# The triangular inverse of a chunked delta-rule scan: 64x64 tiles in a loop against 32x32 tiles written out, with VectorE transposes

## The chip, the cores and the metric

The kernel runs on one core of one Trainium2 chip. The metric is the device time of one execution in microseconds (us). A core has five engines with instruction streams of their own: PE (TensorE, matrix products, which writes PSUM), DVE (VectorE), ACT (ScalarE), POOL (GpSimd) and SP, which here only issues transfers. They meet through semaphores.

## The reference, cut to what matters

The reference is a two-layer hybrid block, then one layer of a second kind (differential attention, a recurrent scan in two directions, and an expert lookup). The change is in the scan alone:

```python
def wkv_scan(s0, scan_in):
    def step(s, inp):
        w, kk, a, k, v, r = inp
        sa = jnp.einsum('dbhij,dbhj->dbhi', s, kk)
        s = s * w[..., None, :] - sa[..., :, None] * (kk * a)[..., None, :] + v[..., :, None] * k[..., None, :]
        return s, jnp.einsum('dbhij,dbhj->dbhi', s, r)
    return lax.scan(step, s0, scan_in)
```

There are 2 directions `d`, 16 heads of width 64, and 256 context plus 256 input tokens, all in float32.

## The kernel before

The scan goes in 8 steps `h` of 64 tokens, steps 0 to 3 over the context and 4 to 7 over the input (`X_STEPS`, which also give outputs). Inside a step the token-by-token recurrence is a triangular system: for each direction and head a 64x64 matrix (I + L), L strictly triangular in time, has to be inverted. The 16 heads lie as 8 column groups `c` times two `head` halves of 64 partitions, so all matrices of a direction fill 128 partitions x 512 columns (8 blocks of 64 columns) of one buffer: `LT` holds the transposed system less the unit matrix, `Dm` the inverse as it grows, `DTm` its transpose (with the two heads' halves swapped), `ARm` the product in between.

The inverse doubles the size of its finished diagonal blocks by levels m = 1, 2, 4, 8, 16, 32 (`LEVELS` = 6). A level has for each direction a "left" product LT' x Dm on PE, a multiplication by a mask on DVE (`tt`, line 2431, reading PSUM), and two products on PE: one gives the new inverse, the other its transpose. Both are copied out of PSUM: lines 2308 and 2312 on ACT, line 2715 on DVE. The first level needs no product: POOL masks it (`begin_inverse`), and ACT makes its transposed copy (`first_transposed`, lines 2298 and 2299). PE's five other levels are a hardware loop (`pe.Fori`, line 1920) with one body of 96 `tile` calls, executed 5 times a step; direction 0 and 1 alternate, so that one's evacuation lies beside the other's products. All matmuls of the scan pass through `mm` (line 1597), therefore have that line; a `tile` call is one 64x64 product.

Around the inverse PE has, written out: `together` (removal and key products), `first_left`, `uncorrected`, then `inverse`; in the next step `corrected_values`, `state_update`, and with outputs `first_outputs`, `last_outputs` and `reads`. The order of each engine is the order of the program text; nothing is scheduled. PSUM banks go through two rings, `act_ring` and `dve_ring`, of four banks each; the inverse holds four banks of the first (`open(pe, "held")`), which needs ACT to have emptied its last two (`evac("U0", ...)`, line 2250).

Of the kernel before, what the change touches and what calls it, by code (L numbers as in the profile page):

```python
# [77 lines left out]
def layout(fields):  # L78
# [10 lines left out]
        ("level", 6 * 128), ("iota16", 16), ("heads", 4)]  # L89
# [38 lines left out]
def constants2():  # L128
# [20 lines left out]
    for m in (1, 2, 4, 8, 16, 32):  # L149
        same = (s[:, None] // (2 * m) == s[None, :] // (2 * m)) & (s[:, None] // m != s[None, :] // m)  # L150
        levels.append(before & same[:, None, :])
    put("level", -1.0 * np.tile(np.stack([m | np.eye(64, dtype=bool)[:, None, :] for m in levels], 1), (2, 1, 1, 1)))
# [178 lines left out]
def build_program(nc, W1, V1, K1, W2_all, VV2, K2, R2, PU, PV, xin, cin, out):  # L331
# [1058 lines left out]
    P_AT, LEVELS = slots_at + 4 * 1024, 6  # L1390
# [25 lines left out]
    def ch2(ap):  # L1416
        return ap.rearrange("p (d c n) -> p d c n", d=2, c=8)

# [90 lines left out]
    inverse_full, inverseT_full = signal("inverse_full", 2 * LEVELS - 2), signal("inverseT_full", 2 * LEVELS - 2)  # L1509
    inverse_ready = signal("inverse_ready", 2 * LEVELS - 2)  # L1510
    inverseT_ready = [signal(f"inverseT_ready{d}", LEVELS - 1) for d in range(2)]
    inverse_done = signal("inverse_done", 2)
# [71 lines left out]
    def _(pe):  # L1584
# [222 lines left out]
        def corrected_values(h, values_of=None):  # L1807
# [3 lines left out]
            for d in range(2):  # L1811
                pe.wait_ge(*inverse_done.at(h, d))
                pe.wait_ge(*u0_ready.at(h, d))
                for c in range(8):
                    for head in range(2):
                        last = tile(b[d], d, c, head, 1, 0, half_of(DTm), half_of(U0))
                        if values_of is not None and c < 7:
                            tile(turned[d], d, c, head, 0, 1, values(values_of), unit)
# [74 lines left out]
        def uncorrected(h):  # L1893
# [4 lines left out]
            for c in range(8):  # L1898
                for head in range(2):
                    tile(b[1], 1, c, head, 0, 1, half_of(Pm), half_of(St), c == 0, False)  # L1900
                    last = tile(b[0], 0, c, head, 1, 1, half_of(Apk), half_of(VT_TOK), c == 0, False)
            pe.wait_ge(*intra_ready.at(h, 1))
            pe.wait_ge(term_full.sem, mark(last))
            for c in range(8):
                for head in range(2):
                    first = tile(b[0], 0, c, head, 0, 1, half_of(Pm), half_of(St), False, True)
                    last = tile(b[1], 1, c, head, 1, 1, half_of(Apk), half_of(VT_TOK), False, True)
            first.then_inc(act_ring.full, 1)
            last.then_inc(act_ring.full, 1)

        def first_left(h, d, left):
            pe.wait_ge(*inverse_begun.at(h, d))
            for c in range(8):
                for head in range(2):
                    last = tile(left[d], d, c, head, 0, 0, half_of(LT), lambda side, d, c: C2["id2"][64 * side:64 * side + 64, :])
            last.then_inc(left_full.sem, 1)

        def inverse(h, left):
            products = [[act_ring.open(pe, "held") for _ in range(2)] for _ in range(2)]
            with pe.Fori(0, LEVELS - 1) as j:  # L1920
                for d in range(2):
                    pe.wait_ge(inverse_ready.sem, j * 2 + ((2 * LEVELS - 2) * h + d + 1))
                    pe.sem_inc(pe_step, 1)
                    for c in range(8):
                        for head in range(2):
                            last = tile(left[d], d, c, head, 0, 1, half_of(LT), half_of(Dm))
                    last.then_inc(left_full.sem, 1)
                for d in range(2):
                    pe.wait_ge(left_ready.sem, j * 2 + ((2 * LEVELS - 2) * h + d + 1))
                    pe.wait_ge(inverseT_ready[d].sem, j + ((LEVELS - 1) * h + 1))  # L1930
                    pe.sem_inc(pe_step, 1)
# [181 lines left out]
    def _(act):  # L2113
# [162 lines left out]
        def token_major_parts(h):  # L2276
# [10 lines left out]
            if h not in X_STEPS:  # L2287
                first_transposed(h, 0)
            removal_tokens(h, 1)
            key_tokens(h, 1)  # L2290
            if h in X_STEPS:
                first_transposed(h, 0)
            first_transposed(h, 1)

        def first_transposed(h, d):
            act.wait_ge(*inverse_begun.at(h, d))
            half = slice(512 * d, 512 * d + 512)
            A(DTm[64:128, half], ARm[0:64, half], ACT.Copy)
            A(DTm[0:64, half], ARm[64:128, half], ACT.Copy)
            act.drain().then_inc(inverseT_ready[d].sem, 1)  # L2300

        def inverse(h):
            banks = act_ring.held(4)
            for j in range(1, LEVELS):
                for d in range(2):
                    if j < LEVELS - 1:
                        act.wait_ge(*inverse_full.at(h, 2 * (j - 1) + d))
                        A(Dm[:, d * 512:(d + 1) * 512], banks[2 * d], ACT.Copy)
                        act.drain().then_inc(inverse_ready.sem, 1)
                    if j == LEVELS - 1 or d == 0:  # L2310
                        act.wait_ge(*inverseT_full.at(h, 2 * (j - 1) + d))
                        A(DTm[:, d * 512:(d + 1) * 512], banks[2 * d + 1], ACT.Copy)
                        act.drain().then_inc((inverse_done if j == LEVELS - 1 else inverseT_ready[d]).sem, 1)
# [107 lines left out]
    def _(v):  # L2421
# [160 lines left out]
        level = C2["level"].rearrange("p (m d t) -> p m d t", m=6, d=2)  # L2582
# [121 lines left out]
        def inverse(h, between):  # L2704
            left, banks = dve_ring.held(2), held_products[h]
            for j in range(LEVELS):
                for d in range(2):
                    if j == 1:
                        v.wait_ge(*inverseT_ready[d].at(h))
# [392 lines left out]
```

## Time and profile before

| | |
|---|---|
| three runs | 2724.05 us median (2721.91 to 2724.41) |
| profiled execution | span 2720.9 us from first to last instruction; no time of its own is given beside the span |
| busy | PE 92%, PE weight loads 63%, DVE 47%, ACT 22%, POOL 19% |
| granted TensorE clock | 0.974 of full over the span |
| the scan | about 1513 to 1888 us of the span |
| instruction transfers (queue q8) | 126 packets, 2.06 MB in the span |

Busy time says how long an engine had an instruction in flight; matmuls are pipelined, so a busy PE isn't PE at its peak. "issue" is idle time for which the profile shows no releaser. The instruction transfers are what brings the engines' programs from memory while they run: 16384 bytes a packet on q8.

### The profile page before, as it was taken

Reading aid. Unit: us, or ns where it says so; the run is one execution under the profiler, and the core shown is the slowest. Engines: PE = TensorE matmul, PEld = TensorE weight load, DVE = VectorE, ACT = ScalarE, POOL = GpSimd, SP = SyncE. Lnnn points to the kernel's source line nnn. Section 1 sums busy time; section 2 is a strip of 40 time slices with the busy share of each in tenths; the row PEclk is TensorE's granted clock in tenths of the full one; section 3 lists DMA queues with packets and bytes.
Section 4 is the critical chain, followed back from the end, with each engine's and each line's share of the span. In section 5 each row is a group of like instructions: output and inputs, shape, how many; then the busy total and the mean of one; then the engine's idle time right before and its main releaser. Section 6 shows DMA issues by size and latency. Waiting matters only on the chain.

```text
span 2720.9 us, 51616 instructions
## 1 busy us (share of the span) xinstructions
PE 2497.1 (92%) x22056; PEld 1706.8 (63%) x22056; DVE 1275.3 (47%) x2865; ACT 598.1 (22%) x1349; POOL 508.4 (19%) x418
## 2 busy tenths in 40 slices
PE   8999999999999999998899988899998988777777
PEld 6688786476886853444677888888866533333333
DVE  2873310037732101146447444444128667777765
ACT  1243000013330000114333444332002111111111
POOL 0000000000000000000012555430003455544552
PEclk9999999999999999999999999999999988988999
DMA  5333343344233335423453111003348999999997
GB/s 186 150 121 124 129 152 152 133 166 155 106 124 139 148 151 212 171 93 124 155 196 83 25 26 34 18 14 122 124 170 329 414 418 421 421 421 422 422 421 308
DMA packets 91234, 523.81 MB, mean 193 GB/s; under 512 B 39728, under 2 KB 39728, under 8 KB 43440
## 3 DMA queue, kind: packets, MB, share of 16 engines
q0 software_dynamic: 39360, 277.51, 25.0%
q1 hardware_dynamic: 51696, 243.80, 24.1%
q8 instruction: 126, 2.06, 0.3%
q14 instruction: 52, 0.43, 0.0%
HBM read 511.85 MB, written 9.44 MB: 192 GB/s over the span
## 4 chain that ended last, share of the span: by engine, by line
PE 70%; DVE 10%; DMA 10%; issue 3%; PEld 3%; ACT 2%; DVEq 1%; POOL 1%; ACTq 0%; PEldq 0%; SPq 0%; POOLq 0%
PE psum L523 35%; PE psum L1597 25%; DMA mem<-weights,mem 9%; PE psum L2055 5%; DVE mem L2924 4%; PEld psum L1597 3%; PE psum L765 2%; PE psum L539 1%; DVE mem L2431 1%; PE psum L2027 1%; DVEq L2552 1%; PE psum L1607 1%; POOL mem L3068 1%; DMA mem<-weights 0%; DVE mem L2568 0%
## 5 line engine op out<-in xcount | busy, mean ns | idle before, releaser
L523 PE MATMUL psum<-mem 128*128 128x256 f32 (+10 forms) x4248 | 954.8, 397 | 7.5 <-DVE mem L1079 3.3
L1597 PE MATMUL psum<-mem 64*64 64x64 f32 (+5 forms) x16032 | 899.8, 258 | 60.8 <-issue 25.6
L1597 PEld LDWEIGHTS psum<-mem 64*64 64x64 f32 (+2 forms) x16032 | 708.6, 144 | 251.3 <-issue 168.0
L523 PEld LDWEIGHTS psum<-mem 128*128 128x128 f32 (+5 forms) x4248 | 692.0, 182 | 262.6 <-issue 168.2
L2055 PE MATMUL psum<-mem 128*128 128x512 f32 x1024 | 497.7, 644 | 123.5 <-ACT mem L2395 121.3
L2055 PEld LDWEIGHTS psum<-mem 128*128 128x128 f32 x1024 | 206.5, 206 | 408.1 <-issue 246.0
L3068 POOL DMA_INDIRECT mem<-weights,mem x256 | 320.3, 1251 | 525.1 <-PE psum L2055 261.2
L2924 DVE CUSTOM_DVE_ANT_0 mem<-mem 128x1024 f32<-128x1024 f32 x256 | 307.4, 1224 | 139.8 <-DMA mem<-weights,mem 133.1
L2431 DVE TENSOR_TENSOR mem<-psum,mem 128x512 f32<-128x512 f32 (+1 forms) x193 | 130.6, 683 | 266.9 <-PE psum L1597 240.4
L2974 POOL TENSOR_TENSOR mem<-mem 128x512 f32<-128x512 f32 (+2 forms) x132 | 168.7, 1294 | 201.0 <-DVEq L2677 150.8
L2431 DVE TENSOR_TENSOR mem<-mem 128x512 f32<-128x512 f32 (+7 forms) x211 | 136.6, 655 | 89.2 <-ACTq L2163 67.5
L2390 ACT ACTIVATE mem<-mem 128x4 f32<-128x4 f32 (+2 forms) x70 | 14.3, 205 | 511.6 <-DVE mem L2928 511.6
L1284 DVE TENSOR_TENSOR mem<-mem 128x512 f32<-128x512 f32 x32 | 22.1, 692 | 193.7 <-ACTq L982 193.7
L1071 DVE SCALAR_TENSOR_TENSOR mem<-mem 128x256 f32<-128x256 f32 x240 | 105.6, 481 | 9.4 <-issue 0.9
L1287 DVE TENSOR_TENSOR mem<-psum,mem 128x512 f32<-128x512 f32 x8 | 5.5, 692 | 205.6 <-PE psum L523 205.6
L1304 POOL DMA_DIRECT2D mem<-vectors x1 | 0.5, 537 | 540.0 <-DVEq L1291 540.0
L1306 POOL MEMSET mem<- 128x256 f32 x1 | 0.3, 311 | 493.9 <-ACT mem L985 493.9
L3031 POOL DMA_DIRECT2D rates_dram<-mem x16 | 14.2, 892 | 406.3 <-DVEq L2600 406.3
L2395 ACT ACTIVATE mem<-mem 128x128 f32<-128x128 f32 x256 | 82.5, 390 | 32.7 <-DVE mem L2431 31.3
L837 ACT ACTIVATE mem<-psum 128x512 f32<-128x512 f32 (+4 forms) x88 | 45.6, 569 | 104.4 <-PE psum L523 100.2
L981 ACT ACTIVATE mem<-psum 128x512 f32<-128x512 f32 x32 | 19.1, 597 | 201.5 <-PE psum L523 201.5
L765 PE MATMUL psum<-mem 128*128 128x512 f32 x128 | 55.8, 594 | 3.8 <-DVEq L1273 3.8
(244 smaller groups left out, 1304.7 us busy)
## 6 DMA issues: line engine op xcount, KB each, us to landing
mem<-weights SPq DMA_DIRECT2D x100, 2048.0 KB, 7.4
rates_dram<-mem POOLq DMA_DIRECT2D x16, 512.0 KB, 4.9
mem<-rates_dram SPq DMA_DIRECT2D x32, 256.0 KB, 4.5
mem<-weights SPq DMA_DIRECT2D x7, 1024.0 KB, 6.8
mem<-weights SPq DMA_DIRECT2D x2, 2176.0 KB
mem<-weights,mem POOLq DMA_INDIRECT x256, 27.4
mem<-weights SPq DMA_DIRECT2D x2, 1536.0 KB, 8.2
mem<-weights SPq DMA_DIRECT2D x2, 1152.0 KB
```

The lines of the kernel that those rows point to most:

```text
L523: ins = pe.matmul(out, lhsT, rhs, start=start, stop=stop, skip_group_check=skip)
L539: last = pe.transpose(b[0:rows_, at:at + n], src, ident[0:n, 0:n])
L765: ins = pe.matmul(b, mg[:, k, t * P:(t + 1) * P], w[half][:, k, :], start=k == 0, stop=k == 7)
L837: return A(dst, src(b) if src else b, func).then_inc(act_ring.free, 1)
L1071: v.scalar_tensor_tensor(cacc[:, c, :], src, w, cacc[:, c, :], ALU.mult, ALU.add)
L1597: ins = pe.matmul(out, lhsT, rhs, start=start, stop=stop, skip_group_check=skip)
L2055: last = pe.matmul(psum[:, 4 + 2 * t + half, :], diag[:, n % DIAGS, :], rows_uv[buf_of[n]][:, D + half * 512:D + (half + 1) * 512], start= ...
L2395: A(diag[:, n % DIAGS, :], ident, ACT.Copy, scale=g1[:, n:n + 1]).then_inc(diag_ready.sem, 1)
L2431: return v.tensor_tensor(o, a, b, op)
L2924: v.tensor_tensor_reduce(u, u, h2[:, t, :], 1.0, 0.0, ALU.mult, ALU.add, actp[:, n:n + 1])
L2974: return pool.tensor_tensor(o, a, b, op)
L3068: pool.indirect_dma_start(out=rows_uv[buf_of[n]], out_offset=None, in_=UV, in_offset=bass.IndirectOffsetOnAxis(ap=eidx_u[:, n:n + 1], axis ...
```

## The change

The last level (m = 32) is taken out of the doubling. The first five (`LEVELS` = 5) act within 32x32 diagonal blocks, so each of them is done on 32x32 tiles: `block_products` makes four calls of `mm` a column group (two heads times two blocks) where `tile` made two, each with 32 rows, 32 columns of weights and 32 moving columns. The buffers `Db`, `DbT` and `ARb` are half as wide (128x256 a direction). The transpose of the inverse, before a second product with a copy out of PSUM, is now a DVE 32x32 transpose of `Db`. PE's loop is gone: its four remaining passes are a Python `for`, written out. The off-diagonal 32x32 block comes from a cross part: two products in a row, with copies by ACT between and behind, and DVE copies of the finished diagonal blocks into `DTm`. `first_transposed` on ACT and POOL's second instruction in `begin_inverse` are gone. `DTm` and `VT_TOK` products keep to their own half (`swapped` arguments 0 in place of 1).

```diff
@@ PE
         def first_left(h, d, left):
             pe.wait_ge(*inverse_begun.at(h, d))
             for c in range(8):
-                for head in range(2):
-                    last = tile(left[d], d, c, head, 0, 0, half_of(LT), lambda side, d, c: C2["id2"][64 * side:64 * side + 64, :])
+                last = block_products(left[d], d, c, block_in(LT, 0), block_unit)
             last.then_inc(left_full.sem, 1)
 
+        def block_products(bank, d, c, lhsT, rhs, block=(0, 1), crossed=0, at=0):
+            for head in range(2):
+                for n in block:
+                    rows_ = block_rows(head, n)
+                    last = mm(bank[block_rows(head, n ^ crossed), at + 32 * c:at + 32 * c + 32],
+                              lhsT(rows_, n, d, c), rhs(rows_, n, d, c), True, True, skip=True)
+            return last
...
-            with pe.Fori(0, LEVELS - 1) as j:
+            for j in range(LEVELS - 1):
                 for d in range(2):
-                    pe.wait_ge(inverse_ready.sem, j * 2 + ((2 * LEVELS - 2) * h + d + 1))
-                    pe.sem_inc(pe_step, 1)
+                    pe.wait_ge(*inverse_ready.at(h, 2 * j + d))
                     for c in range(8):
-                        for head in range(2):
-                            last = tile(left[d], d, c, head, 0, 1, half_of(LT), half_of(Dm))
+                        last = block_products(left[d], d, c, block_in(LT, 0), block_of(Db))
                     last.then_inc(left_full.sem, 1)
                 for d in range(2):
...
                     for c in range(8):
-                        for head in range(2):
-                            one = tile(products[d][0], d, c, head, 1, 0, half_of(DTm), half_of(ARm))
-                            two = tile(products[d][1], d, c, head, 1, 1, half_of(ARm), half_of(DTm))
-                    one.then_inc(inverse_full.sem, 1)
-                    two.then_inc(inverseT_full.sem, 1)
+                        last = block_products(products[d][0], d, c, block_of(DbT), block_of(ARb))
+                    last.then_inc(inverse_full.sem, 1)
+            for d in range(2):
+                pe.wait_ge(*inverse_ready.at(h, 2 * LEVELS - 2 + d))
+                for c in range(8):
+                    last = block_products(products[d][1], d, c, block_in(LT, 1), block_of(Db), (1 - lower(d),), 1)
+                last.then_inc(cross_full.sem, 1)
+            for d in range(2):
+                pe.wait_ge(*cross_ready.at(h, d))
+                pe.wait_ge(*inverseT_ready[d].at(h, LEVELS - 1))
+                for c in range(8):
+                    block_products(products[d][1], d, c, block_of(ARb), block_of(DbT), (lower(d),), 1, at=256)
+                    last = block_products(products[d][1], d, c, block_of(Db), block_unit, (lower(d),), 0, at=256)
+                last.then_inc(cross_full.sem, 1)
@@ ACT
-            first_transposed(h, 1)
...
         def inverse(h):
             banks = act_ring.held(4)
             for j in range(1, LEVELS):
                 for d in range(2):
...
+                    act.wait_ge(*inverse_full.at(h, 2 * (j - 1) + d))
+                    A(Db[:, d, :, :], blocks(banks[2 * d]), ACT.Copy)
+                    act.drain().then_inc(inverse_ready.sem, 1)
@@ DVE
-                    tt(dir_(ARm if j else Dm, d), left[d].rearrange("p (c n) -> p c n", c=8), bc(level[:, j, 1 - d, :], 1, 8), ALU.mult)
+                    tt((ARb if j else Db)[:, d, :, :], blocks(left[d]), bc(level[:, j, 1 - d, :], 1, 8), ALU.mult)
                     v.drain().then_inc((left_ready if j else inverse_ready).sem, 1)
-                if 0 < j < LEVELS - 1:
-                    v.wait_ge(*inverseT_full.at(h, 2 * (j - 1) + 1))
-                    v.tensor_copy(DTm[:, 512:1024], banks)
-                    v.drain().then_inc(inverseT_ready[1].sem, 1)
+                for d in range(2):
+                    if j:
+                        v.wait_ge(*inverse_ready.at(h, 2 * j + d))
+                    v.transpose(DbT[:, d, :, :], Db[:, d, :, :])
+                    v.drain().then_inc(inverseT_ready[d].sem, 1)
                 between(j)
```

PE's program for the inverse of step 1 before, from the last `first_left` to the end of the loop; the loop body stands once in the program and is executed five times. "x15" behind a row is how often it follows itself, the names in brackets are semaphores.

```order
L1597 MATMUL psum<-mem 64x64 [waits inverse_begun,qt_ready]
L1597 MATMUL psum<-mem 64x64 x15
L1920 UNCONDITIONAL_BRANCH [waits act_bank_free]
L1920 ISA
L1597 MATMUL psum<-mem 64x64 [waits inverse_ready]
L1597 MATMUL psum<-mem 64x64 x15
L1922 REGISTER_ALU
L1597 MATMUL psum<-mem 64x64 [waits inverse_ready]
...
L1597 MATMUL psum<-mem 64x64 [waits left_ready,inverseT_ready1]
L1597 MATMUL psum<-mem 64x64 x31
```

The same place in the changed program, from `first_left` through the first of the four passes, which all read like it, and then the cross part.

```order
L1607 MATMUL psum<-mem 32x32 [waits inverse_begun,qt_ready]
L1607 MATMUL psum<-mem 32x32 x31
L1607 MATMUL psum<-mem 32x32 [waits act_bank_free,inverse_ready]
L1607 MATMUL psum<-mem 32x32 x31
...
L1607 MATMUL psum<-mem 32x32 [waits inverseT_ready1,left_ready]
L1607 MATMUL psum<-mem 32x32 x31
...
L1607 MATMUL psum<-mem 32x32 [waits inverse_ready]
L1607 MATMUL psum<-mem 32x32 x15
L1607 MATMUL psum<-mem 32x32 [waits inverse_ready]
L1607 MATMUL psum<-mem 32x32 x15
L1607 MATMUL psum<-mem 32x32 [waits inverseT_ready0,cross_ready]
L1607 MATMUL psum<-mem 32x32 x31
```

A pass is now 128 matmuls in the text, in place of one body of 96 for all five passes; `first_left` has 32 a direction in place of 16, and the cross part adds 96. Counted over the whole program, the scan has 8064 matmuls in the text, before 3712; the branch is gone.

ACT's program before the inverse of step 0, before: the two rows of line 2298 and 2299 twice, ahead of the `evac("U0")` rows of line 2250.

```order
L2262 ACTIVATE mem<-psum 128x512 [waits intra_ready,act_bank_full]
L2298 ACTIVATE mem<-mem 64x512 [waits inverse_begun]
L2299 ACTIVATE mem<-mem 64x512
L2262 ACTIVATE mem<-psum 128x512 [waits lt_ready]
...
L2250 ACTIVATE mem<-psum 128x512 [waits act_bank_full] x2
```

And in the changed program (line 2298 is there `token_half`, line 2286 `evac`, line 2331 the copy of `Db`):

```order
L2298 ACTIVATE mem<-psum 128x512 [waits intra_ready,act_bank_full]
L2298 ACTIVATE mem<-psum 128x512 [waits lt_ready]
L2298 ACTIVATE mem<-psum 128x512 [waits intra_ready,act_bank_full]
L2286 ACTIVATE mem<-psum 128x512 [waits act_bank_full] x2
L2251 ACTIVATE mem<-mem 128x1024 [waits k_ready,rates_landed1]
L2253 ACTIVATE mem<-mem 128x16x64
L2331 ACTIVATE mem<-psum 128x256 [waits inverse_full] x8
```

The copies of the transposed first level no longer stand ahead of `evac("U0")`.

## Rows read from the trace of the kernel before

**Rows 1.** The page: engines, chain by line, largest group, instruction queue
```profile
PE 2497.1 (92%) x22056; PEld 1706.8 (63%) x22056; DVE 1275.3 (47%) x2865; ACT 598.1 (22%) x1349; POOL 508.4 (19%) x418
...
L1597 PE MATMUL psum<-mem 64*64 64x64 f32 (+5 forms) x16032 | 899.8, 258 | 60.8 <-issue 25.6
```

**Rows 2.** Windows, the scan: us, then busy us (instructions), clock, DMA
```profile
1513.00:1888.00 375.00, 332.33 (x13473) 315.44 (x13474) 166.23 (x242) 152.47 (x243) 151.53 (x117) 0.98 0.14 38
```

**Rows 3.** Windows, four loop passes of step 1's inverse
```profile
1571.31:1575.77 4.46, 4.38 (x216) 4.16 (x211) 2.07 (x3) 1.64 (x3) 4.29 (x4) 1.00 0.00 0
...
1584.64:1589.07 4.43, 4.30 (x206) 4.12 (x201) 2.33 (x5) 1.76 (x3) 0.00 (x0) 1.00 0.00 0
sum 17.76, PE 17.16 PEld 16.41 DVE 8.55 ACT 6.98 POOL 8.45; mean PE 4.29 PEld 4.10 DVE 2.14 ACT 1.75 POOL 2.11
```

**Rows 4.** Chain, first pass of that loop: start us, us, what
```profile
1571.79 2.08 PE psum L1597 x64
1573.87 0.07 issue
1573.94 2.09 PE psum L1597 x128
1576.04 0.22 issue
```

**Rows 5.** Transfers by queue, the scan
```profile
q8 instruction: 59, 0.97, 1.1%
```

**Rows 6.** Transfers, 1615 to 1632 us, in 40 slices
```profile
DMA packets 0, 0.00 MB, mean 0 GB/s; under 512 B 0, under 2 KB 0, under 8 KB 0
```

**Rows 7.** Transfers, 1817 to 1833 us, in 40 slices of 0.4 us
```profile
GB/s 0 41 0 0 0 0 0 0 0 0 41 0 0 0 0 0 0 0 0 41 0 0 0 0 0 0 0 0 41 0 0 0 0 0 0 0 41 0 0 0
DMA packets 5, 0.08 MB, mean 5 GB/s; under 512 B 0, under 2 KB 0, under 8 KB 0
```

**Rows 8.** Transfers, 1772 to 1800 us, in 40 slices of 0.7 us
```profile
GB/s 23 0 0 0 0 23 0 0 0 0 0 23 0 0 0 0 23 0 12 0 0 23 0 12 0 0 0 23 0 0 0 0 23 0 0 0 0 23 0 0
q8 instruction: 8, 0.13, 2.0%
```

**Rows 9.** Timeline of PE, 1815 to 1845 us
```profile
1820.06 6.65 PE L1597 MATMUL psum<-mem 64*64 64x64 f32 x254 [0.25 <-issue]
1827.15 3.27 PE L1597 MATMUL psum<-mem 64*64 64x64 f32 x126 [0.45 <-issue]
1830.73 3.11 PE L1597 MATMUL psum<-mem 64*64 64x128 f32 x126 [0.32 <-issue]
1834.25 0.97 PE L1597 MATMUL psum<-mem 64*64 64x64 f32 x49 [0.41 <-issue]
1835.37 1.40 PE L1597 MATMUL psum<-mem 64*64 64x64 f32 x77
1840.59 4.72 PE L1597 MATMUL psum<-mem 64*64 64x64 f32 x111 [3.83 <-issue]
```

**Rows 10.** Waits in the scan: waiter, releaser, us, times, longest us
```profile
PE psum L1597 <- ACT mem L2250: 10.2, 4, 2.6
```

**Rows 11.** Timeline ahead of step 3's inverse
```profile
1647.24 0.63 ACT L2298 ACTIVATE mem<-mem 64x512 f32<-64x512 f32 x1
1647.88 0.63 ACT L2299 ACTIVATE mem<-mem 64x512 f32<-64x512 f32 x1
...
1648.61 1.31 ACT L2250 ACTIVATE mem<-psum 128x512 f32<-128x512 f32 x2
...
1650.36 0.94 PE L1597 MATMUL psum<-mem 64*64 64x64 f32 x18 [2.51 <-ACT mem L2250]
```

**Rows 12.** Groups of the scan: busy us, mean ns, idle before
```profile
L2431 DVE TENSOR_TENSOR mem<-psum,mem 128x512 f32<-128x512 f32 x166 | 113.4, 691 | 154.3 <-PE psum L1597 150.5 <-issue 2.0
L2308 ACT ACTIVATE mem<-psum 128x512 f32<-128x512 f32 x64 | 38.2, 597 | 95.0 <-PE psum L1597 92.0
L2431 DVE TENSOR_TENSOR mem<-mem 128x512 f32<-128x512 f32 (+2 forms) x18 | 21.7, 1221 | 1.8 <-issue 0.7
```

**Rows 13.** The same by form: PE's weight loads and matmuls
```profile
L1597 PEld LDWEIGHTS psum<-mem 64*64 64x64 f32 x13408 | 303.1, 137 | 58.5 <-issue 50.0 <-PE psum L1597 3.3 <-ACTq L2274 1.5
L1597 PE MATMUL psum<-mem 64*64 64x64 f32 x12416 | 286.0, 223 | 38.4 <-issue 19.9 <-ACT mem L2250 10.2 <-PE psum L1597 1.2
...
L1597 PE MATMUL psum<-mem 64*64 64x128 f32 x992 | 38.7, 271 | 4.7 <-issue 4.6
```

More of the change, by code:

```diff
@@ L148, in constants2 @@
     levels = []
-    for m in (1, 2, 4, 8, 16, 32):
+    for m in (1, 2, 4, 8, 16):
         same = (s[:, None] // (2 * m) == s[None, :] // (2 * m)) & (s[:, None] // m != s[None, :] // m)
-        levels.append(before & same[:, None, :])
-    put("level", -1.0 * np.tile(np.stack([m | np.eye(64, dtype=bool)[:, None, :] for m in levels], 1), (2, 1, 1, 1)))
+        level = before & same[:, None, :] | np.eye(64, dtype=bool)[:, None, :]
+        levels.append(np.concatenate([level[:32, :, :32], level[32:, :, 32:]], 0))
+    put("level", -1.0 * np.tile(np.stack(levels, 1), (2, 1, 1, 1)))
     put("iota16", np.tile(np.arange(16), (P, 1)))
@@ L1417, in ch2, with blocks, lower @@
         return ap.rearrange("p (d c n) -> p d c n", d=2, c=8)
+    Db, DbT, ARb = (ap.rearrange("p (d c n) -> p d c n", d=2, c=8) for ap in (Dm[:, 0:512], Dm[:, 512:1024], ARm[:, 0:512]))
+    def blocks(bank):
+        return bank[:, 0:256].rearrange("p (c n) -> p c n", c=8)
+    def lower(d):
+        return 1 - d
     gsig2 = sb2(2048, rtop[0] - 4096).rearrange("p (c t) -> p c t", c=DC)
@@ L1815, in corrected_values @@
                     for head in range(2):
-                        last = tile(b[d], d, c, head, 1, 0, half_of(DTm), half_of(U0))
+                        last = tile(b[d], d, c, head, 0, 0, half_of(DTm), half_of(U0))
                         if values_of is not None and c < 7:
@@ L1905, in uncorrected, with block_rows, block_of, block_in @@
                 for head in range(2):
-                    first = tile(b[0], 0, c, head, 0, 1, half_of(Pm), half_of(St), False, True)
-                    last = tile(b[1], 1, c, head, 1, 1, half_of(Apk), half_of(VT_TOK), False, True)
+                    first = tile(b[0], 0, c, head, 0, 0, half_of(Pm), half_of(St), False, True)
+                    last = tile(b[1], 1, c, head, 1, 0, half_of(Apk), half_of(VT_TOK), False, True)
             first.then_inc(act_ring.full, 1)
             last.then_inc(act_ring.full, 1)
+        def block_rows(head, block):
+            return slice(64 * head + 32 * block, 64 * head + 32 * block + 32)
+        def block_of(buf):
+            return lambda rows_, block, d, c: buf[rows_, d, c, :]
+        def block_in(buf, side):
+            return lambda rows_, block, d, c: ch2(buf)[rows_, d, c, 32 * (block ^ side):32 * (block ^ side) + 32]
+        def block_unit(rows_, block, d, c):
+            return C2["id2"][rows_, 32 * block:32 * block + 32]
+        def block_products(bank, d, c, lhsT, rhs, block=(0, 1), crossed=0, at=0):
[5 more added lines that the diff above has]
+            return last
         def first_left(h, d, left):
@@ L2305, in inverse @@
                 for d in range(2):
[L2306 to L2313, printed above, removed]
+                    act.wait_ge(*inverse_full.at(h, 2 * (j - 1) + d))
+                    A(Db[:, d, :, :], blocks(banks[2 * d]), ACT.Copy)
+                    act.drain().then_inc(inverse_ready.sem, 1)
+            for d in range(2):
+                act.wait_ge(*cross_full.at(h, d))
+                A(ARb[:, d, :, :], blocks(banks[2 * d + 1]), ACT.Copy, scale=-1.0)
+                act.drain().then_inc(cross_ready.sem, 1)
+            for d in range(2):
+                act.wait_ge(*cross_full.at(h, 2 + d))
+                A(ch2(DTm)[:, d, :, 32 * lower(d):32 * lower(d) + 32], blocks(banks[2 * d + 1][:, 256:512]), ACT.Copy)
+                act.drain().then_inc(cross_ready.sem, 1)
             act.sem_inc(act_ring.full, 4)
@@ L2748, in next_rates @@
                     chunk_decay(h + 1)
+            if h == 0:
+                v.memset(DTm, 0.0)
+                v.drain()
             inverse(h, next_rates)
@@ L3016, in begin_inverse @@
         def begin_inverse(h):
-            first = C2["level"].rearrange("p (m d t) -> p m d t", m=LEVELS, d=2)[:, 0, :, :]
             for d in range(2):
```

52 lines of the change are left out of this document (20 added, 32 removed).

## The prediction

> **What bounds the kernel now.** I read the page first: PE is busy 92% of the span and the scan's line 1597 is a third of that, mostly 64x64 tiles [rows 1]. The change touches the scan alone, so I cut it out: 375 us in which PE is busy 332, DVE 166, ACT 152, at a clock of 0.98 [rows 2]. Inside it stand two kinds of PE code, and they are paced by different things.
>
> What is one `tile` call to the engine? By the text the scan executes 3712 matmuls once and the 96 of the body four more times in 8 steps, 6784 in all. The trace has 13408 weight loads and 12416 + 992 matmuls on 64x64 tiles [rows 13], that is two of each for a float32 call, less 1% of missing records. So a call is four instructions. 3712 calls are 14848 instructions; at 64 bytes these are 58 packets of 16384 bytes, and the scan has 59 [rows 5]. The packets are PE's program. In seventeen microseconds of loop none comes at all [rows 6]: a loop runs on what is there.
>
> The written-out code. In 1817 to 1833 us (`first_outputs` to `reads` of the last step) a packet comes every 9 slices of 0.4 us, four gaps in 35 slices: 3.5 us each [rows 7]. In 1772 to 1800 us there are eight, seven gaps in 37 slices of 0.7 us: 3.7 us [rows 8] (the two slices of half height are others'). PE runs in the same beat: 126 matmul records (with their loads 252 instructions, about a packet), a gap with "issue" as its reason, 126 more, and once 3.83 us of nothing [rows 9]. It could go faster: 128 records with their loads, 256 instructions, take 2.09 us in the loop [rows 4]. So written-out tile code here costs about 3.6 us per 256 instructions, not 2.1. Before the change the loop shields the densest part of the scan from that.
>
> **The change part by part.** First the instructions. The text of the scan grows from 3712 to 8064 calls: a step gains 32 in `first_left`, 4 passes x 128 in place of one body of 96, and 96 in the cross part, 544 x 8 = 4352 calls = 17408 instructions = 68 packets.
>
> (1) Removed: four of the five executions of the body in each step, 32 x 4.44 = 142.1 us.
>
> (2) Added: 68 packets of straight code. Bounds per packet: 2.09 us if the program were always there [rows 4]; 3.5 us the quiet beat [rows 7]; 3.7 us in 1772 to 1800 [rows 8]; and 3.95 us as the mean of all written-out scan code with every other wait in it, (375 - 142) / 59 [rows 2, 5]. Inside the inverse the other waits are few, so I take 3.6: 68 x 3.6 = +244.8 us.
>
> (3) The body's first execution stays in the sum as 384 instructions, a packet and a half. It lasts 4.44 us now and will be paced as well: 1.5 x 3.6 = 5.4, +1.0 a step, +8 us.
>
> (4) ACT's copies of the transposed first level go. Ahead of the inverse ACT does two of 0.63 us a direction and only then the `evac("U0")` that frees the banks [rows 11]; PE waits for exactly that 10.2 us, four times up to 2.6 [rows 10], in steps 0 to 3. This wait should vanish, but a gap in PE also lets a packet arrive, so part comes back as pacing: I take -8 (bounds 0 and -10.2).
>
> (5) DVE: eight masks of 0.69 us become halves of that width; the copies become two transposes of 128x256 a pass. No trace row shows a DVE transpose; below, half of a 0.69 us tensor_tensor, 0.35; above, the 1.22 us of one four times as wide [rows 12]. Even so a pass holds 2 x 0.4 + 2 x 1.22 = 3.2 us of DVE against a pass of 2 packets, 7.2 us: nothing. ACT's copies halve too (0.60 to some 0.35) [rows 12]. The four small DVE copies, the memset of step 0, and POOL's dropped instruction lie beside PE. At the cross part PE waits one ACT copy (0.35 and its way) between the products of one direction, with the other's 64 or 128 instructions ahead of it: under 1 us, inside the packet's pace. `corrected_values` now shares the array better with the values' tiles, but it is 256 instructions and so a packet anyway: 0.
>
> Sum: -142.1 + 244.8 + 8 - 8 = **+103 us**. The profiled execution has no time of its own; its span of 2720.9 stands 3.2 under the median of the runs, and I take that margin as unchanged: 2720.9 + 102.7 + 3.2 = **2827 us**, +3.8%.
>
> One rule is weighed here. The trace shows the beat and the gaps [rows 7, 9]. The Trainium skill (Runtime: NRT & Kernel Launch, Instruction fetch mechanics) says that the sequencer streams the program in blocks of 16 KiB (256 instructions), prefetching while it executes, and that crossing a block is "mostly hidden", so that kernels do well to unroll. The block size agrees with the 58 and 59 packets above; the hiding doesn't agree with [rows 9]. By the page the sum would be that of the first rival.
>
> **The rivals.**
> *Fetch hidden, faster.* The dense inverse gets its instructions at the rate of the loop. Then 256 instructions last 2.09 us [rows 4]: a pass of 512 takes 4.2, four 16.7; the cross part 384 instructions, 3.1 plus some 1.0 of turns through ACT; `first_left` 1.0 more. 21.8 against 5 x 4.44 = 22.2 a step, -3; the ACT wait -10.2; and corrected values with free positions, up to -1.4 in seven steps. About -20: 2704 us. For it: nothing shows a packet late in the loop. Against it: [rows 9]. It decides from where a packet costs less than (142.1 + 10) / 68 = 2.2 us; the mean gaps are 3.5 and 3.7, and the shortest one in [rows 7] is 8 slices, 3.2 us.
> *Narrow tiles twice as fast as well.* If besides 32 columns let a stage of 128 instructions end in half its 1.04 us, 16 stages save another 8.3 us a step: some 2640 us. The second stage of [rows 4] speaks against it: with twice the instructions it takes as long as the first, at 8.2 ns an instruction, and their number doesn't fall.
> *The clock drops.* PE waits longer, and the granted clock falls to the lower level, 1.2 GHz, for much of the scan. The paced 32x32 code would hardly mind. The 57 packets of 64x64 work would: 2.09 us of array time doubles to 4.2, past 3.6, +0.6 each, +34: 2861 us. Against: with the gaps of [rows 9] the scan still had 0.98 [rows 2].
> *The stream is slower than its beat*, since transfers of rates and weights crowd it in the inverse, where the loop used to hide that; at 4.2 us a packet, +41: 2868 us.
> *Chain through DVE.* If a transpose took over 3 us a pass would wait for it; 2 us more in 32 passes is +64, 2891 us. Nothing near it in [rows 12].
>
> **How the numbers follow.** Chances: paced at 3.4 to 3.95 us, 0.82; hidden 0.04; hidden and faster tiles 0.01; clock 0.04; slower stream 0.05; DVE chain 0.01; the rest, 0.03, is a partly hidden stream between 2725 and 2790. The likeliest case's bounds: 68 x 3.4 (a tenth under [rows 7]) = 231, less 142.1, less 10.2, is +79, 2803; 68 x 3.95 = 269, less 142.1, plus 8, is +135, 2859. To leave no more than 2 in 10 out I take a little more below, for a stream that gets ahead in PE's other waits: **2795 to 2864**. A measurement here can't tell less than 0.2% (5 us) from no change. Faster by over 0.2%: 0.05; within: 0.01; slower: 0.94.
>
> **What would show it.** In the profile after: q8 packets up by 68, from 126 to about 194; the scan at about 480 us in place of 375; in an inverse a packet every 3.5 to 3.7 us with no pause, some ten a step, a pass at about 7.2 us; PE's idle time before line 1607 "issue" and up by over 100 us; no wait for ACT's `evac` of 2.6 us; a DVE transpose of 0.3 to 1.2 us. Wrong it is if packets come closer than 3.4 us in the inverse (then the beat before was PE's demand, not a limit), if a pass is near 4.2 us, or if passes wait for DVE or ACT by name.

## The result, and the profile after

The changed kernel takes 2850.69 us median (2847.77 to 2852.27, four runs), the kernel before in the same measurement 2724.23 (2721.91 to 2728.85): a ratio of 1.0452, 95% interval 1.0438 to 1.0466. The forecast was 2827 in a range of 2795 to 2864. The profiled execution has a span of 2850.4 us.

The page of the changed kernel, to be read against [rows 1]: engines, granted clock in 40 slices, instruction queue, chain by engine, largest group.

```profile
PE 2482.6 (87%) x24616; PEld 1683.8 (59%) x24616; DVE 1266.1 (44%) x2930; ACT 547.8 (19%) x1301; POOL 486.2 (17%) x402
...
PEclk9999999999999999999997766666999999989999
...
q8 instruction: 194, 3.18, 0.5%
...
PE 64%; DVE 10%; DMA 10%; issue 9%; PEld 3%; ACT 1%; DVEq 1%; POOL 1%; ACTq 0%; PEldq 0%; SPq 0%; POOLq 0%
...
L1607 PE MATMUL psum<-mem 32*32 32x32 f32 (+8 forms) x18592 | 889.2, 264 | 202.2 <-issue 180.2
```

PE is busy for less time than before (2482.6 us against 2497.1) and the span is 130 us longer: the time is idle time of PE, 202.2 us ahead of the matmuls of the line that the scan uses where it was 60.8, and 180.2 of it has no releaser. The queue has 194 packets, 68 more. The windows of the scan up to 2004 us (12 us short of the place at which [rows 2] ends), and in it of one stretch of an inverse; the number behind the engines is the granted clock:

```profile
1513.00:2004.00 491.00, 306.29 (x15970) 284.58 (x15965) 146.47 (x301) 99.93 (x191) 130.81 (x101) 0.66 0.09 22
1586.00:1626.00 40.00, 23.49 (x1238) 22.36 (x1239) 8.19 (x21) 5.42 (x14) 11.05 (x8) 0.51 0.02 4
```

How much longer the scan is shows best at one instruction that both kernels have, VectorE's first behind the products of the last step, before and after:

```profile
1873.16 0.69 DVE L2431 TENSOR_TENSOR mem<-psum,mem 128x512 f32<-128x512 f32 x1 [6.83 <-PE psum L1597]
2001.01 0.69 DVE L2458 TENSOR_TENSOR mem<-psum,mem 128x512 f32<-128x512 f32 x1 [11.37 <-PE psum L1607]
```

It comes 128 us later, nearly the whole of the 130, and PE enters the scan at the same time (1513.01 and 1512.52 us). In the stretch of the inverse DVE (8.2 us of 40) and ACT (5.4) can't be what PE waits for in its 16.5 idle microseconds. PE's timeline there, start and length of each stretch of matmuls, in brackets the idle time before it:

```profile
1587.86 1.93 PE L1607 MATMUL psum<-mem 32*32 32x32 f32 x128 [1.96 <-issue]
1591.70 1.93 PE L1607 MATMUL psum<-mem 32*32 32x32 f32 x127 [1.91 <-issue]
1595.60 1.93 PE L1607 MATMUL psum<-mem 32*32 32x32 f32 x128 [1.97 <-issue]
1599.45 1.92 PE L1607 MATMUL psum<-mem 32*32 32x32 f32 x127 [1.92 <-issue]
```

This is [rows 9] again, but where the gaps before were 0.25 to 0.45 us, they are now as long as the work. 128 records of matmuls with their loads are 256 instructions, one packet; the starts lie 3.84 to 3.90 us apart. The transfers of 1585 to 1615 us, in slices of 0.75 us, have the same beat, a packet every fifth slice and once every sixth:

```profile
GB/s 22 0 0 0 0 22 0 0 0 0 22 0 0 0 0 22 0 0 0 0 22 0 0 0 0 22 0 11 0 0 0 22 0 0 0 0 22 0 0 0
...
q8 instruction: 8, 0.13, 2.3%
```

This stretch is a little slower than the rest. ACT's copies of one direction's inverse follow each other, over the eight steps, by 6.92 to 8.00 us, 7.52 on average: that is a pass of two packets, 3.76 us each.

The waits of the scan say the same by name; the last row is what is left of [rows 10]:

```profile
PE psum L1607 <- issue: 179.1, 109, 3.9
PE psum L1607 <- PE psum L1607: 2.0, 8, 0.8
PE psum L1607 <- ACT mem L2286: 1.9, 2, 1.0
```

### The profile page after: what moved, and what is told of

It reads as the page before. It is cut to its first block, busy times and chain, and to the rows that moved or that the text cites. A ratio compares the mean times of both kernels' runs of the same rounds, so it can differ in the third digit from the quotient of the medians.

```text
span 2850.4 us, 56438 instructions
## 1 busy us (share of the span) xinstructions
PE 2482.6 (87%) x24616; PEld 1683.8 (59%) x24616; DVE 1266.1 (44%) x2930; ACT 547.8 (19%) x1301; POOL 486.2 (17%) x402
## 4 chain that ended last, share of the span: by engine, by line
PE 64%; DVE 10%; DMA 10%; issue 9%; PEld 3%; ACT 1%; DVEq 1%; POOL 1%; ACTq 0%; PEldq 0%; SPq 0%; POOLq 0%
PE psum L524 33%; PE psum L1607 24%; DMA mem<-weights,mem 9%; DVE mem L2957 4%; PE psum L2091 3%; PEld psum L1607 3%; PE psum L766 2%; PE psum L540 1%; DVE mem L2458 1%; PE psum L2063 1%; POOL mem L3096 1%; PE psum L1617 0%; DMA mem<-weights 0%; DVEq L2579 0%; DVE mem L2595 0%
## 5 line engine op out<-in xcount | busy, mean ns | idle before, releaser
L1607 PE MATMUL psum<-mem 32*32 32x32 f32 (+8 forms) x18592 | 889.2, 264 | 202.2 <-issue 180.2
L1607 PEld LDWEIGHTS psum<-mem 32*32 32x32 f32 (+5 forms) x18592 | 688.3, 152 | 402.3 <-issue 319.6
L2091 PE MATMUL psum<-mem 128*128 128x512 f32 x1024 | 493.7, 639 | 128.9 <-ACT mem L2422 128.8
L2458 DVE TENSOR_TENSOR mem<-psum,mem 128x512 f32<-128x512 f32 (+2 forms) x177 | 98.1, 561 | 345.8 <-PE psum L1607 319.0
L3007 POOL TENSOR_TENSOR mem<-mem 128x512 f32<-128x512 f32 (+2 forms) x116 | 147.9, 1295 | 334.8 <-DVEq L2704 280.2
L2741 DVE STREAM_TRANSPOSE mem<-mem 128x256 f32<-128x256 f32 x80 | 35.6, 445 | 107.1 <-ACTq L2332 105.2
L2331 ACT ACTIVATE mem<-psum 128x256 f32<-128x256 f32 x64 | 24.6, 385 | 229.9 <-PE psum L1607 229.9
```

The lines of the kernel that those rows point to most:

```text
L1607: ins = pe.matmul(out, lhsT, rhs, start=start, stop=stop, skip_group_check=skip)
L2091: last = pe.matmul(psum[:, 4 + 2 * t + half, :], diag[:, n % DIAGS, :], rows_uv[buf_of[n]][:, D + half * 512:D + (half + 1) * 512], start= ...
L2458: return v.tensor_tensor(o, a, b, op)
L2741: v.transpose(DbT[:, d, :, :], Db[:, d, :, :])
L3007: return pool.tensor_tensor(o, a, b, op)
```

## The experiments

"Text" is here the program as it stands in memory. Theory: text that TensorE has not run before comes at 3.3 to 3.9 us for 256 instructions, whatever they do, and this sets the time wherever they could run faster. Rivals: the 32x32 tiles themselves are slow (dispatch, array, evacuation), or the lower clock is the cause, or the writing out costs in some other way. Each ratio is to the kernel before, in the same job.

**The loop back, 32x32 tiles kept.**

```diff
-            for j in range(LEVELS - 1):
+            with pe.Fori(0, LEVELS - 1) as j:
                 for d in range(2):
-                    pe.wait_ge(*inverse_ready.at(h, 2 * j + d))
+                    pe.wait_ge(inverse_ready.sem, j * 2 + (2 * LEVELS * h + d + 1))
+                    pe.sem_inc(pe_step, 1)
...
```

> The changed kernel with PE's four passes put back into a hardware loop, still on 32x32 tiles with transposes and the cross part. Pacing by instruction packets: 3 passes x 128 calls x 4 instructions x 8 steps = 48 packets leave the text, so 146 packets on q8; those 24 repeats then run at 3.7 to 4.4 us in place of 7.7 (two packets of 3.85), 2850 - 24 x (3.3 to 4.0) = 2755 to 2771 us, and the granted clock comes back to full in the loop. Rival, the narrow tiles or the lower clock themselves make a pass slow, or its chain through DVE and ACT: a pass stays at 7 us or more and the time above 2840.

Measured: 2733.7 us, ratio 1.0027 (1.0015 to 1.0039), 146 packets. 117 of the 126 us come back by the loop alone, so the tiles are not slow. The time is 21 us below the expected range. The granted clock did not come back to full in the loop as expected: it was 0.84 over the scan. PE's timeline at the loop of one step:

```profile
1575.23 3.82 PE L1607 MATMUL psum<-mem 32*32 32x32 f32 x256 [0.17 <-issue]
1579.23 3.01 PE L1607 MATMUL psum<-mem 32*32 32x32 f32 x256 [0.18 <-issue]
```

Each row is one pass, 256 records. The first ran at a granted clock of 0.50 and started 4.0 us before the next; the second ran at 0.99, and the next starts 3.3 us behind it. The last two passes of the eight loops take 3.37 us on average, 6.6 ns for each of 512 instructions, against 4.44 us of the 64x64 body and 8.2 ns in its second stage. So the tiles are faster than the theory had it, and in a loop, other than in the written-out kernel, the lower clock costs time (in the loops of the whole scan 128 records take 1.9 to 2.2 us at the lower level, 1.4 to 1.7 at the full one). From ACT's first copy of an inverse to its last, the eight steps together take 92 us in place of 181; from the last copy of one inverse to the first of the next, seven times, 244 us in place of 275. So a quarter of the 117 us lies outside the passes. One packet arrives on q8 while each loop runs, which may be what the text behind it gains; no run separates that.

**The loop written out, 64x64 tiles kept** (the same edit on the kernel before).

> The kernel before with its loop written out and nothing else changed: 64x64 tiles, five passes. Pacing: 48 more packets (174 in all), a pass is one and a half packets, 5.3 to 5.8 us in place of 4.44, so 2724 + 40 x (0.9 to 1.4) = 2760 to 2780 us. Rival, writing out is free and the narrow tiles are the cause: the branch's 0.25 us a pass is saved, 2715 to 2724 us.

Measured: 2770.5 us, 1.0161 (1.0140 to 1.0181), 174 packets, clock 0.973 of full, as before the change. Writing out costs 45 us here, with no new tile, no transpose and no lower clock.

**More work for each instruction.** A product moves 64 columns in place of 32; the second half is overwritten by the next column group.

```diff
+            w = 64 if c < 7 else 32
...
+                    last = mm(bank[rows_, 32 * c:32 * c + w], lhsT(rows_, n, d, c), flat[rows_, d, 32 * c:32 * c + w],
+                              True, True, skip=True)
```

> The changed kernel, with 64 moving columns in place of 32 in the products of the four passes; every column beyond the first 32 is overwritten by the next product. Twice the array work in the same number of instructions. Pacing: 194 packets, the same time within 10 us (2840 to 2860), gaps in PE shorter as it is busy for longer. If the lower clock in the inverse is what makes a packet 3.85 us there and not 3.5, and the wider products bring the clock back, some 80 packets x 0.35 less: about 2822 us. Rival, array work sets the passes: they get longer, above 2880 us.

Measured: 2843.0 us, inside the expected range, 1.0436 (1.0413 to 1.0459), an interval that overlaps the changed kernel's. PE's timeline in the inverse of this run:

```profile
1587.70 1.89 PE L1607 MATMUL psum<-mem 32*32 32x64 f32 x128 [1.43 <-issue]
1591.27 1.89 PE L1607 MATMUL psum<-mem 32*32 32x64 f32 x127 [1.68 <-issue]
1594.87 1.89 PE L1607 MATMUL psum<-mem 32*32 32x64 f32 x128 [1.70 <-issue]
1598.43 1.77 PE L1607 MATMUL psum<-mem 32*32 32x64 f32 x119 [1.68 <-issue]
```

A stretch of 256 instructions takes 1.89 us here and took 1.93 before, but not at the same clock: the granted clock is 1.00 in this timeline and was 0.50 in that of the changed kernel. Elsewhere in this run wide stretches at 0.50 show the array's work, and then the gaps shrink:

```profile
1650.04 3.42 PE L1607 MATMUL psum<-mem 32*32 32x64 f32 x127 [1.31 <-issue]
1654.15 3.42 PE L1607 MATMUL psum<-mem 32*32 32x64 f32 x128 [0.69 <-issue]
```

With 1.89 us of work at one level and 3.42 at the other, the beat stays at 3.6 to 4.1 us. The array isn't what paces, though at the lower clock twice the columns come close to it. The clock over the scan rose from 0.66 to 0.88, and the whole is 8 us shorter, which with overlapping intervals is no established gain.

**Half the text of the passes.** Column groups 4 to 7 are left out of the products, masks and copies of the four passes; half of the matrices are not inverted.

```diff
                     pe.wait_ge(*inverse_ready.at(h, 2 * j + d))
-                    for c in range(8):
+                    for c in range(4):
                         last = block_products(left[d], d, c, block_in(LT, 0), block_of(Db))
...
```

> The changed kernel with column groups 4 to 7 left out of the products of the four passes (half the matrices are not inverted), DVE's masks and ACT's copies halved with them; the waits, the stages and their order stay. Pacing: 32 packets fewer (162), a pass is one packet of 3.5 to 3.85 us, 2850 - 32 x 3.85 = 2727 us, at most 10 from it. Rival, a pass is set by its chain of four stages through PE, DVE and ACT with their hand-overs: it shortens only by the array time of half the products, 2850 - 32 x 1.7 / 1 = 2795 us or more.

Measured: 2728.6 us, 1.0017 (1.0000 to 1.0034), 162 packets. 32 packets fewer are worth 122 us, 3.8 each: the beat of the timeline. A turn through DVE and ACT, which has the same number of steps as before, is not what a pass waits for.

**The wait for ACT alone.** On the kernel before, the four copies of the transposed first level are moved behind `evac("U0")`.

```diff
-            first_transposed(h, 1)
...
                 act.drain().then_inc(u0_ready.sem, 1)
+            for d in range(2):
+                first_transposed(h, d)
```

> The kernel before with ACT's two transposed copies a direction moved behind its evacuation of U0, which frees the banks that the loop needs; nothing else. It sizes the term for ACT's wait by itself. The 10.2 us that PE waited for that evacuation in steps 0 to 3 go, if nothing else was late there: 2714 us. If a packet of instructions was on its way meanwhile, part stays as issue: 2718 to 2725. Rival, the copies come too late for the loop's first products, which take their place as the wait: no change, 2724 us or above.

Measured: 2725.9 us, 0.9999 (0.9990 to 1.0009): no change, as the rival expected. The waits of its scan:

```profile
PE psum L1597 <- issue: 34.7, 41, 3.5
PE psum L1597 <- DVEq L2709: 3.5, 4, 0.9
PE psum L1597 <- PE psum L1597: 1.2, 7, 0.2
```

No wait for `evac` is left of the 10.2 us of [rows 10], but 34.7 us have no releaser where [rows 13] had 19.9 ahead of the 64x64 matmuls and 4.6 ahead of the wider ones, and 3.5 are new on DVE (L2709 is the signal behind the mask of an inverse). No wait of PE names the late copies. So PE's time at this place isn't set by ACT's copies alone. That the new idle time is the wait for text, which the old wait had been hiding, is inferred from its having no releaser; the views don't name it.

**VectorE transposes without 32x32 tiles.** The loop over 64x64 tiles, its second product replaced by a DVE transpose of 128x512, with the cross part.

```diff
-                            one = tile(products[d][0], d, c, head, 1, 0, half_of(DTm), half_of(ARm))
-                            two = tile(products[d][1], d, c, head, 1, 1, half_of(ARm), half_of(DTm))
+                            last = tile(products[d][0], d, c, head, 0, 0, half_of(DTm), half_of(ARm))
...
```

> Transposes on VectorE and the cross part as in the changed kernel, but 64x64 tiles (block diagonal matrices) and the four passes in a hardware loop. Text: 32 + 64 + 96 calls a step in place of 128 before, so 8 packets more than before, 134, at 3.75 us each +30; 24 repeats of a pass of two stages of 32 calls. The stages have two of four array positions, so 1.04 us each and 4.4 a pass: 24 x 4.4 in place of 32 x 4.44, -36; ACT's wait up to -10. Sum 2708 to 2722 us. Rival, the chain through a full-width transpose and mask sets a pass, above 5 us: over 2735 us.

Measured: 2734.4 us, 1.0033 (1.0020 to 1.0046), 134 packets. Missed by 12 us, and within 1 us of the rival's mark. In a loop the transpose is not hidden. It takes 711 ns for 128x512, and PE waits 34 times for L2749, which is the signal behind the mask; the mask in turn stands behind two transposes in VectorE's order.

```profile
PE psum L1611 <- issue: 42.7, 39, 4.6
PE psum L1611 <- DVEq L2749: 22.5, 34, 1.4
...
L2753 DVE STREAM_TRANSPOSE mem<-mem 128x512 f32<-128x512 f32 x80 | 56.9, 711 | 50.0 <-ACTq L2344 48.1
```

The chain through one pass shows it:

```profile
1576.08 2.10 PE psum L1611 x64
...
1578.20 0.60 ACT mem L2343
...
1578.85 0.71 DVE mem L2753
...
1579.68 0.69 DVE mem L2470
...
1580.64 2.10 PE psum L1611 x64
```

Yet a pass lasts only 4.56 us (1576.08 to 1580.64) where 4.4 was expected, so over all 32 passes this is 5 us. The forecast also had up to 10 us for ACT's wait, which the run before showed to be worth nothing; without it the sum is 2718, and some 11 us stay open.

**Less text, with loops.** Four kernels take calls out of the straight part. The first two leave out the 32 unit products a step that carry the diagonal blocks through the cross part (DVE copies them instead):

```diff
-                    block_products(products[d][1], d, c, block_of(ARb), block_of(DbT), (lower(d),), 1, at=256)
-                    last = block_products(products[d][1], d, c, block_of(Db), block_unit, (lower(d),), 0, at=256)
+                    last = block_products(products[d][1], d, c, block_of(ARb), block_of(DbT), (lower(d),), 1, at=256)
```

With 32x32 tiles:

> The loop on 32x32 tiles (first experiment, 2734 us) without the 32 products with the unit matrix in each step's cross part; VectorE copies those finished diagonal blocks instead. 4 packets fewer, 142 on q8. Pacing: 4 x 3.75 = 15 us less, about 2719 us. Rival, only engine work counts, and the cross part waits for its copies anyway: the products took 0.85 us of PE a step at most, so 2727 us or no change.

Measured: 2723.9 us, 0.9989 (0.9977 to 1.0001), 142 packets; 10 us under the run with the loop back, between the two expectations. With 64x64 tiles:

> The kernel of loops over 64x64 tiles with VectorE transposes (2734.4 us, 134 packets) without the unit products of the first block copies, which VectorE makes. 32 calls a step fewer are 4 packets fewer (130 on q8). If each packet is worth 3.7 us, 2719 us; if only the wait of the passes for the VectorE transposes counts, which stays as it is (22 us in 34 waits), 2730 us or more.

Measured: 2718.9 us, 0.9974 (0.9962 to 0.9986), 130 packets, as the packets expect. The wait behind mask and transposes stayed (22.3 us in 33 waits), yet 15.5 us went.

The other two also take `first_left` off PE: GpSimd masks the first level into the transposed buffer, VectorE transposes it. The edit as the 32x32 kernel has it; with 64x64 tiles it is one mask into `DTm` and a transpose into `Dm`:

```diff
+                for n in range(4):
+                    rows_, at = slice(32 * n, 32 * n + 32), 32 * (n % 2)
+                    ptt(DbT[rows_, d, :, :], ch2(LT)[rows_, d, :, at:at + 32], bc(first[rows_, d, :], 1, 8), ALU.mult)
                 pool.drain().then_inc(inverse_begun.sem, 1)
...
+                v.wait_ge(*inverse_begun.at(h, d))
+                v.transpose(Db[:, d, :, :], DbT[:, d, :, :])
```

With 64x64 tiles:

> The loop on 64x64 tiles with transposes, without the unit products, and with the first level made by POOL's mask and a VectorE transpose in place of PE products with the unit matrix. Text: 64 + 64 calls a step, as many as before, so 126 packets; 24 repeats of 4.4 us. Pacing: 8 packets fewer than the kernel with transposes in the loop, 30 us: 2680 to 2695 us, faster than before by 30 to 45. Rival, the first level's way through POOL and VectorE lies open, some 2 us a step: 2700 to 2710 us.

Measured: 2712.6 us, 0.9961 (0.9946 to 0.9976), 126 packets. This is above both ranges, 2.6 us over the rival's: PE now waits for the first level's way through GpSimd and VectorE, 9.4 us in 4 waits at the head of an inverse, and 4 packets fewer than in the run before gained only 6 us. With 32x32 tiles:

> The kernel with loops over 32x32 tiles and without unit products (2723.9 us, 142 packets on q8), with the first level made from four masks of 32 partitions on GpSimd into the buffer DbT and a VectorE transpose, in place of 64 matmul calls a step. The theory that packets on TensorE's queue set the time expects 8 packets fewer (134 on q8) and about 3.7 us for each, so some 2694 us. The rival, that the way through GpSimd and VectorE opens at the head of an inverse (as the waits of 9.4 and 12.8 us did in the run of the 64x64 kernel without a first level on TensorE, 2712.6 us), expects 2703 to 2712 us, with a wait of PE or DVE for the masks or their transposes in the chain.

Measured: **2697.7 us**, 0.9899 (0.9885 to 0.9913), 134 packets: 1.0% under the kernel before and the fastest of all, 4 us from what the pacing theory expects and 5 below the rival's range. Its waits in the scan:

```profile
PE psum L1607 <- issue: 58.1, 63, 3.7
PE psum L1607 <- DVEq L2736: 10.1, 5, 2.1
PE psum L1607 <- ACT mem L2284: 5.4, 3, 1.8
```

The head of an inverse does wait here too (10.1 us; L2736 is the signal behind the transpose of the first level), but narrow transposes keep the passes free of VectorE.

**How much text may stand in a loop.** The four 32x32 passes as two executions of a body of two passes, 1024 instructions.

```diff
-            with pe.Fori(0, LEVELS - 1) as j:
-                for d in range(2):
+            with pe.Fori(0, (LEVELS - 1) // 2) as j:
+                for i in range(2):
+                    for d in range(2):
...
```

> The changed kernel with its four passes as a hardware loop of two passes a body, executed twice: 1024 instructions in the body, where the loop of one pass has 512 (2733.7 us, 146 packets) and the written-out program 2048 (2850.7 us, 194 packets). The text grows by 128 calls a step over the loop of one pass, 512 instructions, 16 packets in all. If each packet of text brought costs what the 48 of the full writing out cost, (2850.7 - 2733.7) / 48 = 2.44 us, this run has 162 packets and some 2773 us. If the body no longer fits into what PE keeps of its program, it is brought for each execution: 194 packets and some 2850 us. A rival in which writing out costs by something else than the text (the waits with constants, the loop's increments) expects 2734 us.

Measured: 2778.4 us, 1.0189 (1.0175 to 1.0204), 162 packets; forecast 2773. One inverse on PE's timeline:

```profile
1580.77 1.95 PE L1607 MATMUL psum<-mem 32*32 32x32 f32 x125 [2.00 <-issue]
1584.57 1.95 PE L1607 MATMUL psum<-mem 32*32 32x32 f32 x126 [1.85 <-issue]
1588.29 2.06 PE L1607 MATMUL psum<-mem 32*32 32x32 f32 x126 [1.77 <-issue]
1592.40 6.92 PE L1607 MATMUL psum<-mem 32*32 32x32 f32 x484 [2.05 <-issue]
1599.74 3.52 PE L1607 MATMUL psum<-mem 32*32 32x32 f32 x282 [0.42 <-DVEq L2740]
```

Here both regimes stand side by side. The first execution of the body limps, 126 records and 1.8 to 2.0 us of nothing. From its last hundred records on, through the branch and most of the second execution, 484 records run in 6.92 us without a break. Same instructions and the same engines beside them, and much the same granted clock (0.54 over the three slow stretches, 0.59 over the fast one): the difference is whether the text has been there.

## Why the prediction was right, point by point

*What bounds the kernel, and step (2)*, hold. 68 packets were forecast and 68 came; removing text in the passes (3.8 us a packet for 32) and keeping it in a loop (117 us for 48) move the time, and more array work for each instruction doesn't. The size was short: 3.6 us was taken from two windows of straight code, where the packets of [rows 2] that come within 4.3 us of each other lie 3.75 us apart on average, and the passes of the changed kernel ran at 3.76 a packet (7.52 us a pass where 7.2 were forecast). Steps (2) and (3) together price 68 + 12 = 80 packets, so this is 13 us. With the 8 us of step (4), below, it makes 21 of the miss of 24 us.

*Step (1)*, 142 us removed, can't be seen alone, but it fits: the scan ended 128 us later, and -142 + 80 x 3.76 - 8 x 4.44, the last for the first execution that step (3) prices anew, = +123. The forecast for the scan was about 480 us; 375 and 128 are 503.

*Step (3)*, the first execution paced as well, is what the timeline of the loop of two passes shows.

*Step (4)* failed: the wait for ACT was given -8 and is worth nothing. It went (10.2 to 1.9 us), but the run that took it away alone was no faster (0.9999), and idle time without a releaser had taken its place there. Its bound of 0 was the right value; the doubt stood in the step ("part comes back as pacing"), only the part was all.

*Step (5)* holds in the written-out kernel: the transpose takes 445 ns, inside its bounds of 0.35 and 1.22, and no wait of PE names DVE.

```profile
L2741 DVE STREAM_TRANSPOSE mem<-mem 128x256 f32<-128x256 f32 x80 | 35.6, 445 | 107.1 <-ACTq L2332 105.2
L2458 DVE TENSOR_TENSOR mem<-psum,mem 128x256 f32<-128x256 f32 x80 | 34.0, 425 | 108.5 <-PE psum L1607 107.1
L2331 ACT ACTIVATE mem<-psum 128x256 f32<-128x256 f32 x64 | 24.6, 385 | 229.9 <-PE psum L1607 229.9
```

The cover of that zero was the slow text: with 64x64 tiles in a loop the wider transposes stand in the chain of every pass, and a pass lasts 4.56 us. The 2 us a pass of the last rival are far from it.

*The rivals.* That the text is hidden (2704 us) is out by every written-out run. That narrow tiles are faster as well was half right as a mechanism and had no effect: 3.37 us a pass against 4.44, seen only in a loop. The prediction's argument against it, 8.2 ns an instruction whatever the tile, is refuted by 6.6 ns.

The clock did fall, as the third rival said, which had a chance of 0.04: the granted clock of the scan was 0.66 in place of 0.98, its lower level of 1.2 GHz for some 41 us in each inverse, after PE had begun to idle for half of its time. That it would hardly touch the paced 32x32 code was right too. Stretches of 256 instructions took 1.93 us there, and between packets closer than 4.3 us in the scan the mean was 3.77 us at the lower level (77 of them) and 3.75 at the full one (20): the text, not the clock, paces. The +34 of this rival rested on 64x64 work outside the inverse, where the clock had mostly recovered. No run changes the clock alone; what these show is that the packets came no slower at the lower level.

Of the signs of being wrong one came in part: 8 of the 126 intervals between packets were under 3.4 us (the shortest 3.30). The mean stood well above it.

*The rule of the Trainium skill* (Runtime: NRT & Kernel Launch, Instruction fetch mechanics) that crossing a block is "mostly hidden", and that kernels prefer full unrolling where possible (for the sake of its taken branches, not of the crossing, as the prediction puts it), goes against these runs where the instructions are short: unrolled, the same passes cost 45 us (64x64) and 117 us (32x32). Its size of a block agrees: 16384 bytes a packet, 256 instructions.

**What stays open.** Why a packet takes what it takes was not settled: 3.75 us on average in the scan of both kernels, 3.84 to 3.90 in the stretch shown, 3.63 in the run with wide products at the full level. Nor does a packet have one price: 3.8 us where text of the passes went with its work, 2.8 and 2.3 where text replaced executions of a loop (45 us for the first 16 packets, 72 for the next 32), since the loop's executions took time as well. In the four kernels with less text it was 2.4 to 3.9 a packet except from 130 to 126, where 6 us came for four. Whether the new wait at the head took the rest there was not tested.

## What to carry to other kernels

Count the instructions of a written-out stretch and divide by 256: where that many packets at some 3.7 us exceed its work, the text is the bound, and neither smaller tiles nor faster helpers gained anything here. Put such stretches in a hardware loop, even one of two executions, and take out calls that only copy; a float32 call costs four instructions on 32x32 tiles as on 64x64. The best kernel here is only 1.0% under the one before, so look first at what share of the whole such stretches have. A wait that ends while the next packet is still on its way may be worth nothing, so price a removed wait together with what paces the engine next.

## What the hardware showed that was not expected

A loop body of 1024 instructions was kept: its second execution ran without a pause (the last timeline), and the queue had no more packets than the text is long. 256 instructions on 32x32 tiles with 32 moving columns took 1.93 us at a granted clock of 0.50, with 64 moving columns 1.89 us at 1.00 and 3.42 at 0.50. A float32 transpose on VectorE took 445 ns for 128x256 and 711 for 128x512, close to a tensor_tensor of the same size (425 and 691). The granted clock fell to 1.2 GHz in a stretch where PE was 59% busy (23.5 of 40 us), and the beat of the packets didn't show it; in a loop on the same tiles it did, 3.82 us a pass of 256 records against 3.01.
